# Other places for the sample batches among the projection's half tiles, and the transpose back ahead of the next keys

## The reference

```
z = rmsnorm(x) @ W_in
A: attention, 6 heads of 64; windows and dilations (128,1), (512,4), (2048,16), merged by denominators
B: depthwise convolution and a gated linear recurrence (RG-LRU)
C: gated linear recurrence with a matrix state (HGRN2), 6 heads
y = x + concat[A * silu(g_A), B * silu(g_B), C * silu(g_C)] @ W_out ; final rmsnorm(y)
```

```python
kg = jnp.take(k_all, idx, axis=1)                     # the keys of a branch, window // dilation + 1 of them
scores = jnp.einsum('bthd,btnhd->bthn', q, kg) * (dh ** -0.5)
p = jnp.exp(scores - mx)
o = jnp.einsum('bthn,btnhd->bthd', p, vg) / l
```

## Time and profile before

| | |
|---|---|
| median of 3 runs | 1998.87 us (1997.27 to 2001.96) |
| the profiled execution | 1998.87 us, span 1997.1 us |
| PE busy | 1823.2 us (91%) |
| VectorE, ACT, POOL busy | 996.4, 871.5, 648.6 us |
| mean granted clock of PE | 0.955 of full |
| DMA | 162.16 MB, mean 81 GB/s |

### The profile page before, as it was taken

How to read it: one execution, slowest core, us unless ns; L and a number is a source line. 1 busy time by engine, 2 the same in 40 slices (tenths; PEclk the granted TensorE clock), 3 DMA queues, 4 the chain that set the end, 5 groups by cost and what they waited for, 6 DMA issues and landing times. The chain is left out here.

```text
span 1997.1 us, 30088 instructions
## 1 busy us (share of the span) xinstructions
PE 1823.2 (91%) x10924; PEld 1600.9 (80%) x10924; DVE 996.4 (50%) x2046; ACT 871.5 (44%) x1642; POOL 648.6 (32%) x882
## 2 busy tenths in 40 slices
PE   5999988999999999999999995358989998999998
PEld 5988878899999999999999894247778886666665
DVE  3437644224666666666665503444545546454542
ACT  3438762114655556555655412266556532111110
POOL 1103211004565555565555302033333341212110
PEclk9999989999999999999999996568999999999999
DMA  5310111222021202111111114571241066475641
GB/s 191 93 46 33 42 50 50 67 96 72 23 61 26 59 22 57 30 44 36 26 56 28 49 46 111 112 164 41 54 104 43 14 190 188 149 219 165 195 143 53
DMA packets 181774, 162.16 MB, mean 81 GB/s; under 512 B 65434, under 2 KB 168891, under 8 KB 180859
## 3 DMA queue, kind: packets, MB, share of 16 engines
q1 hardware_dynamic: 181626, 160.24, 28.1%
HBM read 116.89 MB, written 46.55 MB: 82 GB/s over the span
## 5 line engine op out<-in xcount | busy, mean ns | idle before, releaser
L49 PE MATMUL f_bank<-f_ht,f_whi 128*128 128x384 f32 (+2 forms) x1080 | 402.8, 373 | 5.7 <-DVE f_wlo L824 5.7
L51 PE MATMUL f_bank<-f_ht,f_wlo 128*128 128x384 f32 (+2 forms) x1080 | 382.7, 354 | 0.0
L50 PE MATMUL f_bank<-f_ht,f_whi 128*128 128x384 f32 (+2 forms) x1080 | 382.6, 354 | 0.0
L776 ACT ACTIVATE f_scr<-f_scr 128x384 f32<-128x384 f32 (+1 forms) x210 | 114.5, 546 | 271.6 <-POOL f_scr L562 271.3
L49 PEld LDWEIGHTS f_bank<-f_ht,f_whi 128*128 128x128 f32 x1080 | 204.5, 189 | 19.6 <-DVE f_wlo L824 6.5
L50 PEld LDWEIGHTS f_bank<-f_ht,f_whi 128*128 128x128 f32 x1080 | 204.8, 190 | 13.1 <-issue 1.4
L51 PEld LDWEIGHTS f_bank<-f_ht,f_wlo 128*128 128x128 f32 x1080 | 203.8, 189 | 13.1
L1129 PE MATMUL f_tps<-f_scr 128*128 128x128 f32 x1536 | 205.5, 278 | 2.3 <-DVE f_scr L966 2.3
L1129 PEld LDWEIGHTS f_tps<-f_scr 128*128 128x128 f32 x1536 | 194.7, 193 | 5.2 <-DVE f_scr L966 2.5
L966 DVE TENSOR_TENSOR f_scr<-f_scr 128x192 f32<-128x192 f32 (+1 forms) x210 | 101.0, 482 | 180.5 <-ACT f_scr L776 180.1
L561 POOL TENSOR_TENSOR f_scr<-f_scr 128x192 f32<-128x192 f32 (+1 forms) x210 | 133.9, 638 | 84.2 <-PE f_tps L1129 81.7
(11 more groups left out here) (382 smaller groups left out, 3635.8 us busy)
## 6 DMA issues: line engine op xcount, KB each, us to landing
f_wraw<-in_w_in SPq DMA_DIRECT2D x27, 512.0 KB, 4.2
a_raw<-zf SPq DMA_DIRECT2D x48, 256.0 KB, 4.2
zt<-f_stage SPq DMA_DIRECT2D x48, 192.0 KB, 1.8
a_k<-in_ck SPq DMA_DIRECT2D x48, 192.0 KB, 3.6
a_v<-in_cv SPq DMA_DIRECT2D x48, 192.0 KB
f_scr<-in_xp SPq DMA_DIRECT2D x16, 512.0 KB, 4.1
a_x<-in_xp SPq DMA_DIRECT2D x16, 512.0 KB, 4.5
out_y_prompt<-a_y SPq DMA_DIRECT2D x16, 512.0 KB, 2.9
```

The costliest lines, as they stand in the source:

```text
L49: nc.tensor.matmul(out, w_hi, m_hi, start=start, stop=False)
L50: nc.tensor.matmul(out, w_hi, m_lo, start=False, stop=False)
L51: return nc.tensor.matmul(out, w_lo, m_hi, start=False, stop=stop)
L776: A(lev[i % 3][:, :n], lev[i % 3][:, :n], ACT.Exp).then_inc(S["expd"], 1)
```

## The change

Three edits: the batches stand at 3, 6, 9, 12, 16, 19, 22 and 26; where `sb` of a batch and `sk` of the next fall on one half tile, `sb` comes first; and `entries` lists each batch's seven entries (K0, K1, K2, Q, N, F, B) in one go, with B last.

```diff
--- before.py
+++ after.py
@@ -1526,7 +1526,7 @@
 
 
 
-    first = [32 * b // 10 + 4 for b in range(NB)]
+    first = [33 * b // 10 + 3 for b in range(NB)]
     at = {}
     for b, s in enumerate(first):
         for step, kind in enumerate(("sk", "sm", "so")):
@@ -1546,10 +1546,10 @@
             order.append(("pt", 1))
         if s == 1:
             order.append(("sq", 0))
+        if at.get(s - 1, ("",))[0] == "so":
+            order.append(("sb", at[s - 1][1]))
         if kind:
             order.append((kind, b))
-        if at.get(s - 1, ("",))[0] == "so":
-            order.append(("sb", at[s - 1][1]))
         order.append(("pe", s))
         if s < 3:
             order.append((("si", "sj", "sl")[s], 0))
@@ -1790,13 +1790,8 @@
         rows_of = lambda i: P if i < NTILE else NS
 
         entries = [("T", 0), ("Q", 0)]
-        for kind, b in order:
-            if kind == "sk":
-                entries += [("K0", b), ("K1", b), ("K2", b)] + [("Q", b + 1)] * (b + 1 < NB)
-            elif kind == "sm":
-                entries += [("N", b), ("F", b)]
-            elif kind == "sb":
-                entries.append(("B", b))
+        for b in range(NB):
+            entries += [("K0", b), ("K1", b), ("K2", b)] + [("Q", b + 1)] * (b + 1 < NB) + [("N", b), ("F", b), ("B", b)]
 
         def bank(kind, b):
             return ring[entries.index((kind, b)) % 2]
```

## The result

The changed kernel takes 2017.82 us in the median (2011.73 to 2023.12), the one before 1998.07 (1995.58 to 2002.0). The medians differ by 19.8 us. The direction and the places were as forecast, the size was not: 12.7 us were forecast, and 2017.82 lies above the range of 2005 to 2016.

A forecast was written before the change was run, and what follows sets the result against it. PE's order and waits were taken to bound the last stage. 0.6 (batch 0) + 7.3 (waits on B) + 0.1 + 0.2 (small waits) + 4.5 (clock) = 12.7 on 1998.87, so 2011.5 us; range 2005 to 2016.

The forecast's parts named there:

- What bounds the stage: Last stage: PE always busy, so only its order and waits count; a new order alone wins at most 4.7 us.
- Batch 0: Its key block moves ahead of `pp` 4; PE idles 5.5 us at the far scores instead of 4.7; +0.6 us.
- The waits on B: Second key transpose, batches 1, 3, 6: PE idles 2.6 us until VectorE reads B; net +2.4 each, +7.3 us.
- Odd half tiles: Batches 2 and 5: second key transpose waits 0.1 us at most, +0.1 for both; far-score waits elsewhere add +0.2.
- The clock after these gaps: Behind each new 2.6 us gap, some 3.2 us of PE work at clock 0.50, 1.5 us lost, three times: +4.5.
- What rides along: POOL's product of batch 1 runs earlier and may hold VectorE; batch 0's `sm` stays hidden with 1.3 us to spare.
- Sum: All terms on the profiled execution's 1998.87 us: +12.7 us, so 2011.5 us; chance 0.55.
- The second: Rival: behind each new gap the clock falls for twice as long, as after 1114.75; 2016.5 us, chance 0.09.

The follow-up runs named there:

- Run 7: Kernel before the change, with VectorE's 17 mask operations (9.2 us) issued ahead of half tile 0 instead of after half tile 1; 1989.4 us, ratio 0.9967.
- run 2: Kernel before the change, with the transpose back ahead of the next keys and B last in the list, batches at the old places; 2012.04 us, ratio 1.0078.
- run 3: Changed kernel, but B is written into the bank of the sum `o` and is no entry of the list; 2001.59 us, ratio 1.0022.
- run 4: Changed kernel, with PE's four idle gaps filled by 128x384 products whose result is not used; 2002.65 us, ratio 1.003.
- run 5: Changed kernel plus 24 unused 128x384 products behind the wait of the second key transpose at batches 1, 3 and 6; 2022.34 us, ratio 1.013.
- run 9: Changed kernel plus 36 full fp32 transposes of 128x128 behind each wait on B at batches 1, 3 and 6; 2023.02 us, one profile.
- run 12: Changed kernel plus 12 full fp32 products of 384 columns, 48 weight columns, behind each wait on B; 2031.81 us, one profile.
- run 11: Changed kernel plus 72 full fp32 products of 16 columns, 48 weight columns, behind each wait on B; 2049.34 us, one profile.
- run 10: Changed kernel as it is, profiled a second time for the lengths at the lower clock; 2021.81 us.
- run 6: Kernel before the change, with POOL's product of the far keys cut into 6 parts of 128x384; 1998.07 us, ratio 1.0004.

## Why the prediction was wrong, point by point

- *What bounds the stage, and that an order can win 4.7 us at most.* Right. Run 7 wins that and the clock behind it.
- *Batch 0.* The new wait was forecast at 5.5 us, to 1678.75; it is 5.58, to 1678.79. The cost was forecast at +0.6 us and is +3.2: `sm` 0's transposes, the same point of the work, begin at 1693.24, and `pp` 4 ended at 1690.03 before with the same done. The rest of the key block took 6.28 us and `pt` 3 with `pp` 4 took 8.17 (1685.07 to 1693.24), where 3.36 and 6.6 are full speed, so 4.5 us were lost to the clock and not 2.0. Right in mechanism, the clock mis-sized.
- *The waits on B.* Three, at batches 1, 3 and 6, released by the two products behind the reduction: right. 7.1 us of idle time against 7.8 (3 x 2.6; 7.3 net of the waits for the far scores that they replace). Runs 2, 3 and 4 show it each in its way.
- *Odd half tiles.* No wait, and 0.17 us longer transposes, twice; forecast 0.1 for both. The far scores wait 0.15 us at half tile 26 and not at all at 16, which is no more than before; the forecast had +0.2.
- *The clock after these gaps.* **This term failed.** The prediction took "some 3.2 us of work at the lower level: 3.2 x 0.47 = 1.5 us, three times: +4.5". Measured are, beyond full speed, 3.85 in the key block and 0.8 in the half tile behind it at batch 1, 1.5 at batch 3, and 4.9 and 1.1 at batch 6: 12.1 us. The price of each us was right: at batch 1 4.6 us were lost in 10.1 us at 0.50, 0.46 for each. The length was wrong, and the reason is in what I compared with: the two gaps of the earlier trace rows and the one of the earlier trace rows were followed by dense work with many columns. Here the key block follows, with products of 8 and 16 columns in it. Runs 5, 9 and 12 put dense work there and get 3.3 us or nothing, run 11 puts products of 16 columns there and gets 13.6 to 17.0. The upper bound I gave, 3 x 6.7 us, was drawn from the same rows and too low as well. That the clock fell behind all three gaps was forecast from five of five in one execution. The trace has a sixth such gap, 2.88 us to 1300.69, with 17.1 us at 0.50 behind it and further gaps in these; but the gap near 470 us, one of the five, is followed by a fall in only half of the 14 profiles. So this part came true with some luck.
- *What rides along.* The earlier product did not delay `sm` 0: PE shows no wait there. Right.
- *Sum.* 3.2 + 7.1 + 12.1 + 0.3 = 22.7 of the 23.2 us between the two profiled executions. By the ratio it is 18.8: the changed kernel's runs spread over 11 us, and the profiled one is among the slowest, so in most executions the times at the lower level may be shorter than in this trace. Of the 18.8 the waits are 8.0 (run 4), as forecast, and the clock is 10.8, where 4.5 were forecast.
- *The rivals.* The second, twice as long at the lower level, had 0.09 and 2016.5 us; it came nearest, but its reason (a longer time whatever follows) was not the one.

**Left open.** Batch 3 in the changed kernel (and batches 2 and 7 in run 2) came off with 3.3 us though the same block follows. The table behind run 10 shows that these are the cases in which the level fell 0.3 to 0.8 us after the wait's end; why it fell there, and why this makes it short, no run shows. The same holds for the five gaps in runs 5, 9 and 12 without a fall: the added work also moved them in time, and no run moved a gap by itself.

## What to carry to other kernels

A list that shares two banks in turn ties each entry to the one two places ahead: before moving an entry in it, look for who will read that neighbour and what this reader has queued in front. A short idle time of PE, here 2.3 to 2.4 us, can be paid twice, once as a wait and again as clock, and in this kernel the second price went with the work behind it: ahead of dense products the lower level lasted at most 3.4 us (some 1.5 us lost), in front of the key block 1.5 to 6.0 us were lost. So if PE must wait, look whether it can wait ahead of wide products that are there anyway (adding them only for this did not pay, run 5), or fill the gap (run 4: the clock stayed at 1.00 from 1660 to 1990 us); and look first for work that a late engine can do in an earlier idle stretch, as the 9.2 us of masks here.

## What was not expected of the hardware

- The lower level lasted 13.6 to 17.0 us behind unbroken products of 16 columns, and 3.3 us or nothing behind ones of 128 or 384 columns in the same type (runs 9, 11, 12). At batch 1, where the level fell 1.1 to 1.3 us after the end of the same gap each time, it was 13.7 us behind 16 columns, 10.2 before the key block and 3.4 behind 128 or 384 columns.
- With dense work right behind them, five of nine gaps of 2.3 to 2.4 us brought no fall at all (two each in runs 5 and 12, one in run 9). The five counted in the trace of before had each been followed by one, but one of these, near 470 us, was so in only 7 of 14 profiles, with the same work around it.
- The gap of 4.1 us near 285 us was followed by 6.8 us at the lower level in 7 of the 14 profiles and by 3.4 in the other 7; it was 6.8 where the level fell 0.6 us or more before the gap's end.
- POOL's product in six parts took 8.24 us beside a busy VectorE, 5.12 in one piece; the four VectorE operations of the split took 0.8 us more each (run 6). But it can take longer in one piece too: 7.68 us for batch 1's in the changed kernel, which started 0.7 us behind a scaling on VectorE, and the scaling was not held (1.27 us).
